# A hybrid decoder trunk on one core: x's second half turned later, gates and feed-forward joined in another order, value heads finished on VectorE alone

## The reference

```
h += 0.5 * post_norm(SwiGLU_1(pre_norm(h)))
h += post_norm(mixer_i(pre_norm(h)))         # layer 0: hybrid; layer 1: latent attention
h += 0.5 * post_norm(SwiGLU_2(pre_norm(h)))
h += post_norm(sigmoid(pre_norm(h) W_g) * (p[i] W_p))
```

```
mu = mean(x); xc = x - mu; var = mean(xc * xc)
y = xc * rsqrt(var + 1e-5) * g + b
```

## Time and profile before

| what | value |
|---|---|
| median of 3 runs | 1157.87 us (1157.59 to 1159.87) |
| the profiled execution | 1159.81 us |
| its span | 1158.1 us |
| mean granted clock of TensorE | 0.992 |
| TensorE busy | 1120.5 us, 97% |
| TensorE weight loads busy | 947.1 us, 82% |
| VectorE busy | 815.1 us, 70% |
| ScalarE busy | 564.8 us, 49% |
| GpSimd busy | 97.9 us, 8% |
| bytes moved | 205.73 MB, 178 GB/s mean |

### The profile page before, as it was taken

One profiled execution on the slowest core, in us unless ns is written; L12 is line 12 of the kernel. 1 busy time (PEld: TensorE's weight loads), 2 busy tenths in 40 slices (PEclk: granted clock), 3 DMA queues, 4 the chain that ended last, 5 costly groups with the idle time before them and its releaser, 6 DMA issues. The chain is left out here.

```text
span 1158.1 us, 14172 instructions
## 1 busy us (share of the span) xinstructions
PE 1120.5 (97%) x5775; PEld 947.1 (82%) x5775; DVE 815.1 (70%) x1036; ACT 564.8 (49%) x691; POOL 97.9 (8%) x125
## 2 busy tenths in 40 slices
PE   8999999999899999999989999999889999999997
PEld 5888888788787788888867888888788878888885
DVE  5776777579787677667756777767755567776775
ACT  7444345467453554434545544346554555434443
POOL 3000000202500200000023000001200020000002
PEclk9999999999999999999999999999999999999999
DMA  9555555645333465555553555554512446555541
GB/s 315 217 182 186 201 195 182 241 158 182 109 128 109 156 253 183 192 199 189 182 218 123 211 187 194 201 182 152 212 48 99 146 145 231 198 198 182 184 179 55
DMA packets 30848, 205.73 MB, mean 178 GB/s; under 512 B 3664, under 2 KB 3696, under 8 KB 7616
## 3 DMA queue, kind: packets, MB, share of 16 engines
q1 hardware_dynamic: 27648, 194.00, 47.2%
q0 software_dynamic: 3136, 10.83, 2.9%
HBM read 203.77 MB, written 1.05 MB: 177 GB/s over the span
## 5 line engine op out<-in xcount | busy, mean ns | idle before, releaser
L171 DVE TENSOR_TENSOR WL<-raw,WH 128x2048 fp32r<-128x2048 f32 x181 | 414.9, 2298 | 165.5 <-ACT WH L164 165.1
L164 ACT ACTIVATE WH<-raw 128x2048 fp32r<-128x2048 f32 x181 | 344.9, 1908 | 127.6 <-DMA raw<-stream 127.6
L582 PE MATMUL PS<-X,WH 128*128 128x512 f32 x1152 | 288.2, 392 | 0.0
L582 PEld LDWEIGHTS PS<-X,WH 128*128 128x128 f32 x1152 | 209.1, 189 | 38.8
L585 PEld LDWEIGHTS PS<-X,WL 128*128 128x128 f32 x1152 | 157.2, 190 | 11.2
L585 PE MATMUL PS<-X,WL 128*128 128x256 f32 x1152 | 160.6, 282 | 0.0
L189 PE MATMUL PS<-WH,X 128*128 128x512 f32 (+1 forms) x352 | 140.6, 399 | 9.3 <-DVE WL L171 5.6
L684 ACT ACTIVATE sgb<-sgb 128x256 f32<-128x256 f32 x72 | 30.1, 418 | 229.5 <-DVE sgb L680 229.5
L190 PE MATMUL PS<-WH,X 128*128 128x512 f32 (+1 forms) x352 | 137.6, 391 | 0.0
L191 PE MATMUL PS<-WL,X 128*128 128x512 f32 (+1 forms) x352 | 137.5, 391 | 0.0
L189 PE MATMUL PS<-WH,BH 128*128 128x512 f32 x288 | 113.1, 393 | 0.0
(11 more groups left out here) (273 smaller groups left out, 1343.7 us busy)
## 6 DMA issues: line engine op xcount, KB each, us to landing
raw<-stream SPq DMA_DIRECT2D x181, 1024.0 KB, 4.8
PG<-post_g POOLq DMA_DIRECT2D x8, 512.0 KB, 6.4
QG<-pre_g POOLq DMA_DIRECT2D x7, 512.0 KB, 7.2
raw<-stream SPq DMA_DIRECT2D x4, 512.0 KB, 7.3
h<-x SPq DMA_DIRECT2D x2, 512.0 KB, 5.6
out<-h SPq DMA_DIRECT2D x4, 256.0 KB, 2.1
wsT<-gm_w POOLq DMA_DIRECT2D x1, 512.0 KB, 10.0
gm_g<-gm_g POOLq DMA_DIRECT2D x1, 512.0 KB, 8.1
```

The costliest lines, as they stand in the source:

```text
L164: act.activation(WH[:, n % RING, :], raw[:, n % RING, :], ACT.Copy).then_inc(sem("w_hi"), 1)
L171: dve.tensor_tensor(WL[:, n % RING, :], raw[:, n % RING, :], WH[:, n % RING, :], ALU.subtract).then_inc(sem("w_lo"), 1)
L582: pe.matmul(PS[:, bank, :], wh[:, kt, cols], X[:, kt, :, :].rearrange("p a n -> p (a n)"), start=kt == 0, stop=False)
```

## The change

Five things are changed.

1. **Half transposes.** In a feed-forward that follows the hybrid or the attention, and in the hybrid stage, tile 1's first half of x is turned before quarter 2 of block (2,0), its second half before block (0,1). The attention stage already did it so.
2. **From the gates to feed-forward 2.** The first half of tile 0's x is turned inside gate block (2,1), the second inside (3,1), no longer behind the gates. The feed-forward starts with (0,0), (1,0), (2,0), (3,0), (0,1), (1,1), (2,1), (3,1); tile 1's first half is turned in (3,0). ScalarE loads its sigmoid table and takes the sigmoids with one unit less split ahead; the units m+1, m+2 and m+3 are split between the parts of the boundary. VectorE makes unit m+1's low half between the two low halves of tile 0's x, and unit m+3's between tile 1's mean and its update of h.
3. **Value heads.** VectorE does it all in two `scalar_tensor_tensor` per head: (v - mean) * gain, then * reciprocal root + shift. GpSimd's four products are gone.
4. **Order of VectorE in the hybrid stage.** Unit 14's low half comes between the two statistics, unit 15's before the first tile is normalised; the second tile is normalised behind unit 16's half and xd.
5. **CL.** `out_low` of tile 1 comes before the low halves of units 24 and 25.

The diff, cut:

```diff
@@ boundary_act
-            split_to(m + 2)
-            x_high(act, s, 0)
+            if stages[s - 1][0] == "ple":
+                x_high(act, s, 0, (0,))
+                split_to(m + 1)
+                x_high(act, s, 0, (1,))
+                split_to(m + 2)
+            else:
+                split_to(m + 2)
+                x_high(act, s, 0)
             post_square(act, s - 1, 1)
+            if stages[s - 1][0] == "ple":
+                split_to(m + 3)
             pre_square(act, s, 0)
@@ boundary_dve
-            split_to(m + 1)
+            from_ple = stages[s - 1][0] == "ple"
+            split_to(m if from_ple else m + 1)
             behind(dve, s - 1, 0)
...
-            x_low(dve, s, 0)
+            x_low(dve, s, 0, (0,))
+            if from_ple:
+                split_to(m + 1)
+            x_low(dve, s, 0, (1,))
             if stages[s][0] != "mla":
                 split_to(m + 2)
-            behind(dve, s - 1, 1)
+            behind(dve, s - 1, 1, (lambda: split_to(m + 3)) if from_ple else None)
@@ ffn_start_pe
-            order = lagged(range(4), 2) if s else [(j, t) for j in range(4) for t in range(2)]
-            for j, t in order:
+            lead = 0 if not s else 3 if stages[s - 1][0] == "ple" else 2
+            for j, t in lagged(range(4), lead):
...
+                if s and (j, t) == (0, 1):
+                    transpose_x(pe, s, 1, (1,))
...
-                    if s and (j, t) == (2, 0) and q % 2 == 0:
-                        transpose_x(pe, s, 1, (q // 2,))
+                    if s and (j, t, q) == (lead, 0, 2):
+                        transpose_x(pe, s, 1, (0,))
@@ ple_pe
-            for t in range(2):
-                for j in range(1 - t, 4):
-                    gate(j, t)
+            for j in range(1, 4):
+                gate(j, 0)
+            turn_next = next_x(pe, s)
+            gate(0, 1)
+            gate(1, 1)
+            gate(2, 1, turn_next and (lambda q: q == 1 and turn_next(0)))
+            gate(3, 1, turn_next and (lambda q: q == 0 and turn_next(1)))
@@ ple_act
-            split_to(first[s] + 6)
+            split_to(first[s] + 4)
             load_table(act, ACT.Sigmoid)
+            split_to(first[s] + 5)
@@ hyb_pe
-                    if (idx, j, t) == (1, 0, 0) and q % 2 == 0:
-                        transpose_x(pe, s, 1, (q // 2,))
+                    if (idx, j, t, q) == (1, 0, 0, 2):
+                        transpose_x(pe, s, 1, (0,))
...
+                    if (n, t) == (0, 1):
+                        transpose_x(pe, s, 1, (1,))
@@ hyb_dve, normalise(c)
                 dve.wait_ge(sem("hy_mv"), c + 1)
+                if c == 0:
+                    dve.wait_ge(sem("hy_gm"), 32)
+                for r in range(8):
+                    cols = slice(r * P, (r + 1) * P)
+                    m = 8 * c + r
+                    ins = dve.scalar_tensor_tensor(vt[:, c, cols], vt[:, c, cols], MV[:, 2 * m:2 * m + 1], gm_g[:, cols],
+                                                   ALU.subtract, ALU.mult)
+                chain(ins)
                 dve.wait_ge(sem("hy_rv"), c + 1)
                 for r in range(8):
-                    v = vt[:, c, r * P:(r + 1) * P]
+                    cols = slice(r * P, (r + 1) * P)
                     m = 8 * c + r
-                    ins = dve.tensor_scalar(v, v, MV[:, 2 * m:2 * m + 1], RV[:, m:m + 1], ALU.subtract, ALU.mult)
-                ins.then_inc(sem("hy_vn"), 1)
+                    ins = dve.scalar_tensor_tensor(vt[:, c, cols], vt[:, c, cols], RV[:, m:m + 1], gm_b[:, cols],
+                                                   ALU.mult, ALU.add)
+                ins.then_inc(sem("hy_v"), 1)
@@ hyb_dve, order
             head_statistics(0)
+            split_to(u + 14)
             head_statistics(1)
-            split_to(u + 14)
             times_dt(0)
+            split_to(u + 15)
             normalise(0)
-            normalise(1)
-            split_to(u + 15)
             split_to(u + 16)
             times_dt(1)
+            normalise(1)
...
-            split_to(u + 24)
+            split_to(u + 23)
+            out_low(1, 8, "hy_yhi", "hy_ylo")
             split_to(u + 25)
-            out_low(1, 8, "hy_yhi", "hy_ylo")
@@ hyb_pool: affine(0) and affine(1) are gone
@@ tensor program
-                if s == 0 or stages[s - 1][0] == "ple":
+                if s == 0:
                     transpose_x(pe, s, 0)
```

More of the change, by code:

```diff
@@ L329, in update_h, with behind @@
                                      ALU.mult, ALU.add).then_inc(sem("h_new"), 1)
-        def behind(dve, s, t):
+        def behind(dve, s, t, between=None):
             if stages[s][0] == "ple":
@@ L338, in behind @@
             post_mean(dve, s, t)
+            if between is not None:
+                between()
             dve.wait_ge(sem("post_rs"), 2 * s + t + 1)
@@ L389, in x_high, with x_low @@
                 act.activation(x_half(XH, t, a_), x_psum(s, t, a_), ACT.Copy).then_inc(sem("x_hi"), 1)
-        def x_low(dve, s, t):
-            for a_ in range(2):
+        def x_low(dve, s, t, halves=(0, 1)):
+            for a_ in halves:
                 dve.wait_ge(sem("x_hi"), 4 * s + 2 * t + a_ + 1)
@@ L795, in projected, with gate @@
                 wide(pe, u, t, 4 + 2 * t, p_hi, p_lo, 0, True, True, middle=middle)
-            def gate(j, t):
+            def gate(j, t, middle=None):
                 if j == 0:
                     x_there(pe, s, t, 1)
-                wide(pe, u + 1 + j, t, 2 * t, XH, XL, 2 * j, j == 0, j == 3, "ple_gate" if j == 3 else None)
+                wide(pe, u + 1 + j, t, 2 * t, XH, XL, 2 * j, j == 0, j == 3, "ple_gate" if j == 3 else None, middle)
             pe.wait_ge(sem("p_lo"), i + 1)
@@ L898, in hybrid_trunk @@
                      "hy_da", "hy_acs", "hy_acv", "hy_dea", "hy_dte", "hy_back", "hy_xs", "hy_xd", "hy_bc",
-                     "hy_bt", "hy_cbm", "hy_abc", "hy_seg", "hy_exp", "hy_G", "hy_mv", "hy_skip", "hy_rv", "hy_vn", "hy_v", "hy_t0",
+                     "hy_bt", "hy_cbm", "hy_abc", "hy_seg", "hy_exp", "hy_G", "hy_mv", "hy_skip", "hy_rv", "hy_v", "hy_t0",
                      "hy_mix", "hy_mixv", "hy_ya", "hy_trya", "hy_yahi", "hy_yalo", "hy_yd", "hy_st", "hy_stv",
@@ L1495, in skip @@
                     .then_inc(sem("hy_skip"), 1)
-            def affine(c):
-                if c == 0:
-                    pool.wait_ge(sem("hy_gm"), 32)
-                pool.wait_ge(sem("hy_vn"), c + 1)
-                link(pool, "pool_chain", pool.tensor_tensor(vt[:, c, :], vt[:, c, :], gm_g[:, :], ALU.mult))
-                pool.tensor_tensor(vt[:, c, :], vt[:, c, :], gm_b[:, :], ALU.add).then_inc(sem("hy_v"), 1)
-            affine(0)
-            affine(1)
             skip(0)
@@ L2165, in _ @@
             for s, (kind, _) in enumerate(stages):
-                if s == 0 or stages[s - 1][0] == "ple":
+                if s == 0:
                     transpose_x(pe, s, 0)
-                if s == 0:
                     idle_products(pe, 8)
```

## The result

| | before | after |
|---|---|---|
| median | 1158.78 us (1157.59 to 1159.87, 4 runs) | 1145.2 us (1143.31 to 1146.08, 4 runs) |
| ratio, 95% interval | | 0.9881 (0.9862 to 0.99) |
| profiled execution, span | 1159.81, 1158.1 us | 1146.08, 1144.4 us |
| mean granted clock | 0.992 | 0.996 |

The time was forecast at 1144.7 us. Run again later beside other kernels, the changed kernel took 1144.8 us (ratio 0.9874, 0.986 to 0.9889).

The account below looks back on a forecast made before the run. TensorE (97% busy) was taken as the bound, its gaps mostly at stage boundaries and mid-hybrid; 0.2 + 4.0 + 1.4 + 7.6 = 13.2 us off gave 1144.7 us by the median, range 1141.2 to 1149.2.

Parts of the forecast that it names:

- part 2: Value heads and VectorE's order in the hybrid stage: 4.0 us gained, bounds 0.9 (skips and reciprocal root block fully) and 6.3.
- Part 1: Half transposes into hybrid stage, feed-forwards 1 and 3: waits for hn give way to waits at (3,0); 0.2 us gained.
- rival 3: Part 1 gives all it removes, the weight half keeping ahead: plus 3.4 us, 1141.3 us; chance 0.07.
- rival 1: Hybrid stage: GpSimd fully in VectorE's way, part 2 brings 0.9 us, clock falls again; 1149.3 us; chance 0.14.
- Part 3: Near the hybrid stage's end: out_low before unit 24's half makes CL earlier; 1.4 us gained, bounds 1.0 and 1.5.
- Part 4: Gates to feed-forward 2: earlier sigmoids, transposes inside the gates, two smaller new waits; 7.6 us gained, bounds 4.5 and 10.2.
- Rival 2: Gates to feed-forward 2: the new wait for unit m+3 grows, part 4 brings 4.5 us; 1148.0 us; chance 0.10.
- rival 5: Gates: sigmoids come no earlier, held by something else in ScalarE's queue; only 5.6 us gained, 1152.3 us; chance 0.04.
- Rival 4: VectorE becomes the hybrid stage's bound and the kernel slower, new instructions needing 0.68 us each; 1162 at 0.8; chance 0.02.

Follow-up runs that it names:

- undo_half: Changed kernel with only the half transposes undone in the hybrid stage and feed-forwards 1 and 3; 1145.78 us.
- split_first: Changed kernel with VectorE making unit m+3's low half between the two low halves of tile 1's x, at three boundaries; 1141.51 us.
- pe_late: Changed kernel with only TensorE's part of the gates change undone: tile 0's transposes stand behind the last gate block again; 1151.05 us.
- skips_late: Changed kernel with GpSimd's two skip products waiting until VectorE has finished the second tile's heads; 1144.33 us.
- order_only: Changed kernel with VectorE's new hybrid order but the old operations: 16 tensor_scalars on VectorE, gain and shift on GpSimd; 1143.82 us.

## Why the prediction was right

The mechanism was right in all four parts: the waits that were to go are gone, and the new ones stand where they were expected. That the total came within 0.5 us is in part luck, since one execution of this kernel differs from another by more than that, in part 2 and in the attention stage.

**Part 1** (0.2 us for three boundaries): 0.1, 0.1 and nothing by undo_half's rows. The wait of 1.08 became one of 0.84 at unit m+3's low half, where 1.0 was forecast; rival 3 is excluded by its presence in all three places (0.84, 0.85 and 0.86). What the step had not seen is that in the hybrid even the full removal is worth nothing (split_first), since VectorE is late further on.

**Part 2** (4.0 us): 4.4 by the markers of the first profile, about 3.1 by those of the second. Unit 15's wait is gone. The new waits, 1.96 and 0.86 (2.53 and 0.86 in the second), are in the range of 1 to 3. The mechanism, GpSimd's skips getting in between the new instructions, was right; its course was not: both got into tile 0, not one there and one behind xd, and they held VectorE for 3.3 us, where 2.7 were counted. With 3.3 the step's own sum, 6.3 less what GpSimd takes, gives 3.0, and the second profile has it. The 4.4 of the first come from 1.2 us by which VectorE's statistics started earlier, for which the step had no term: the weights of one unit came sooner. (In the profiles of the experiments the statistics begin at 276.27 to 277.28.) Unit 15's half, due at 287.5, was there at 286.3 in the first profile and at 287.6 in the second. There is one profile of the kernel before, so how its own start varies isn't shown. The reciprocal root, the third item of rival 1, held nobody: it ran from 283.43 for 1.67 us, and the low half that began at 284.04 took its usual 2.28. With that, with part 2 at 3.1 or more and with a granted clock of 1.00 behind the new waits, rival 1 is out. What the step put together and the experiments took apart is that the order brings the gain and the new operations cost part of it. The undisturbed group of eight, put at 2.2 us from a row of other work, measured 2.17 to 2.2.

**Part 3** (1.4 us): 1.38.

**Part 4** (7.6 us): 7.7. Unit m+3's wait is 1.65 (2.0 forecast), the silu's 0.24 (0.5), and the last transposes wait for nothing. Rivals 2 and 5 are excluded by these rows. (Rival 2's own sum is 0.2 us off: 4.5 for part 4 gives 1147.8.) The working priced transposes and sigmoids as one. By pe_late the earlier sigmoids remove the wait for hn, and 3.5 of the 7.7 us come only with the placing inside the gates.

**Rival 4** never came near: it needed 0.68 us for each new instruction; the disturbed ones take 0.48 (3.83 for eight).

The Trainium skill (SBUF — State Buffer, section Who interferes with whom) says that a VectorE instruction with two SBUF inputs and a GpSimd instruction that reads SBUF exclude each other for the whole instruction, and that a VectorE instruction with one SBUF input outside its two-port modes does not. Most rows agree: eight scalar_tensor_tensors of 3.83 beside a skip and of 2.19 without; statistics of 1.64 us beside a reciprocal root of 1.68. One pair does not: the reciprocal root of 1.67 us at 283.43 was still under way when the low half, which has two SBUF inputs, began at 284.04, and the half took its usual 2.28. Part 2 lies above the lower bound of 0.9 mainly for that reason: it had counted both skips and the root in full, and only the skips were paid (3.3 of 3.8 us).

## What to carry to other kernels

A wait is only worth removing where the engine that ends it isn't late again further on: follow its chain to the next place it is waited for, as the hybrid's boundary showed (0.84 us removed, nothing gained). Try an order and the operations that come with it apart: here the order was worth 6.9 us by the medians (6.5 by the rows, 383.15 against 376.69) and the operations cost 1 to 3 us. And work that must not meet another engine's, like GpSimd's products with two-input VectorE work, belongs into that engine's own waits, each named by a semaphore, not merely later in its queue.

## What the runs showed that I had not expected

- **Who comes in between.** A skip issued during a 2.28 us low half got in as soon as that half ended, ahead of the first scalar_tensor_tensor (285.08, 3.01 us long, of which 1.9 are its work). Before, between two low halves back to back, one was kept out to the end of the second (293.81, 6.59 us). I have no run that tells why.
- **Small GpSimd work is held too.** An addition on 128x8 takes 0.24 to 0.26 us beside statistics or xd, but 2.19 when it starts right behind the start of a low half (skips_late; the same in the changed kernel):

```profile
279.17 2.26 DVE L171 TENSOR_TENSOR WL<-raw,WH 128x2048 fp32r<-128x2048 f32 x1
279.34 2.19 POOL L1519 TENSOR_SCALAR sm<-sm 128x8 f32<-128x8 f32 x1 [65.79 <-DVE sm L1341]
```

- **A tensor_scalar with one SBUF tile as input is held as well:** eight took 5.29 us beside GpSimd's affine products and 2.14 without (order_only). Whether it runs in one of the two-port modes, which the section named above sets apart, no row tells.
- **The clock behind the same wait isn't the same from run to run.** The attention stage waits 2.0 us for cn in every kernel. The changed kernel's first profile has 0.50 behind it, its second one 1.00 (window view, granted clock behind the engines):

```profile
801.00:804.00 3.00, 3.00 (x9) 2.32 (x8) 1.78 (x4) 1.84 (x2) 1.00 (x2) 0.50 0.85 328
```

```profile
801.00:804.00 3.00, 2.43 (x12) 1.75 (x11) 2.41 (x2) 2.82 (x7) 0.00 (x0) 1.00 0.45 101
```

  From the transposes ahead of that stage to unit m+3's wait behind it the first took 144.05 us (790.09 to 934.14), the second 140.90 (791.85 to 932.75). About half of that lies further on: from 826 to 840 us the granted clock is 0.88 in the first and 1.00 in the second. So a single profile of this kernel carries 3 us that are no property of it. The profile of before has the lower level behind this wait too, so the table of markers compares like with like:

```profile
815.00:818.00 3.00, 3.00 (x9) 2.33 (x8) 1.78 (x4) 1.57 (x1) 1.01 (x2) 0.53 0.80 333
```

  In the hybrid stage the second lost 1.3 us in turn: VectorE's statistics begin at 277.61 against 276.29, since ScalarE waited 1.64 us for the weights of the split at 225.82 and 0.30 for the one at 224.47.
